# A gated attention block on one core: both MLP products as seven-product block products

## The chip, the cores and the metric

The kernel is one program on one NeuronCore of a Trainium2 chip; the other cores are idle. The metric is the time of one execution in device microseconds. Of the core's engines, PE does the matmuls, DVE (vector) and ACT (scalar) read and write both SBUF and the eight PSUM banks, POOL (GpSimd) works on SBUF only, and SP issues the DMA transfers.

## The reference

One decoder layer over 1024 tokens (SEQ) of 1024 channels (D), all in float32. First comes a mixing half: RMS norm, projections, differential attention and a pooling mixer, gates, and an output projection `w_o`, added to `x`. The MLP follows:

```python
h2 = rms_norm(x, norm2_g[l])
u = jnp.square(jax.nn.relu(jnp.einsum('bsd,df->bsf', h2, w_mlp_in[l])))
x = x + jnp.einsum('bsf,fd->bsd', u, w_mlp_out[l])
```

The inner width FF is 4096, so each MLP product is 1024 x 1024 x 4096.

## The kernel before

**Precision.** Each float32 operand is kept as two float32r parts: `hi` is the copy that ACT writes, and `lo` is the rest, which DVE gets by subtracting (`split_hi` L495, `split_lo` L776). `passes` (L1135) makes three matmuls of each pair: hi x hi, lo x hi, hi x lo. Each matmul has 128x128 weights and 512 moving columns and adds into one PSUM bank.

**Output projection.** `out_projection(t)` (L1378) handles one tile of 128 tokens: 2 halves of output columns x 8 blocks of k x 3 matmuls. Its operand is `featT`, the split of `mergedT`: ACT's `merged_hi` (L701), DVE's `merged_lo` (L1055), and POOL for the first tile (L488). DVE adds the result to the residual `res` (L1082), which lies in SBUF as 8 tiles loaded from x. ACT squares it (L734), POOL makes the inverse root (L413, L415), DVE the norm `h2_row` (L1094), and PE transposes it (`h2_transpose` L1395) two tiles later; ACT and DVE split the transposed tile into `featT` (L728, L1074).

**MLP.** FF is cut into 8 chunks of 4 blocks of 128. `mlp_up(c)` (L1413) computes, for each block j and each half i of the tokens, 8 blocks of k x 3 matmuls. ACT applies Relu and Square (L754, L759), DVE squares once more and takes the low part (L1103, L1106); the result `uT` stays in SBUF. `mlp_down(c)` (L1430) computes, for each tile of tokens and each half of output columns, 4 blocks x 3 matmuls, and DVE adds them to `res` (L1116). The weights come in blocks of 512 KB through four `raw` tiles (`load` L316, `load_chunk` L339) and are split once (L500, L779).

**Order.** Each engine has its own queue, written out by hand, with loops over chunks; semaphores connect them. SP's queue is in order too, so a transfer behind a wait goes out only when the wait ends.

Of the kernel before, what the change touches and what calls it, by code (L numbers as in the profile page):

```python
# [24 lines left out]
F32 = mybir.dt.float32  # L25
F32R = mybir.dt.float32r
# [8 lines left out]
def trunk_layer(nc, x, norm1_g, w_in, b_gate, q_norm_g, k_norm_g, lam_params, subln_g,  # L35
# [33 lines left out]
    with ExitStack() as ctx:  # L69
# [50 lines left out]
        res = at("res", 64, [P, T, D])  # L120
        h2_row = [at(f"h2_row{i}", 144 + 4 * i, [P, D]) for i in range(2)]
        g2_row = at("g2_row", 152, [P, D])
        square2 = at("square2", 156, [P, D])

        uT = (at("uT_hi", 144, [P, CH, SEQ], F32R), at("uT_lo", 96, [P, CH, SEQ], F32R))
        relu = [at(f"relu{i}", 208 + 2 * i, [P, HT]) for i in range(2)]
        u_full = [at(f"u_full{i}", 212 + 2 * i, [P, HT]) for i in range(2)]
# [7 lines left out]
        in_hi = at("in_hi", 128, [P, 2, BLOCK], F32R)  # L135
        in_lo = at("in_lo", 136, [P, 2, BLOCK], F32R)
        slots = [(slot_hi[:, i], slot_lo[:, i]) for i in range(4)]
        slots += [(more_hi[:, i], more_lo[:, i]) for i in range(4)]
        slots += [(in_hi[:, i], in_lo[:, i]) for i in range(2)]
# [36 lines left out]
        def sem(name):  # L176
# [7 lines left out]
        res_in = sem("res_in")  # L184
# [130 lines left out]
        def _(sp):  # L315
# [22 lines left out]

            def load_chunk(c):  # L339
                for i, (kind, j) in enumerate(MLP_ORDER):  # L340
                    if kind == "in":
                        load(i % 4, mlp_in_v[:, :, bass.ds((c * CH + j) * P, P)], MLP0 + 8 * c + i)
                    else:
                        load(i % 4, mlp_out_v[:, bass.ds(c * CH + j, 1), :], MLP0 + 8 * c + i, parts=1)
# [36 lines left out]
            sp.wait_ge(up_full, 4 * KD)  # L381
            for t in range(T):
                sp.dma_start(res[:, t, :], x_rows[t]).then_inc(res_in, 16)
# [4 lines left out]
            load_chunk(0)  # L388
            with sp.Fori(1, CHUNKS) as c:
                load_chunk(c)  # L390
            for t in range(T):
                sp.wait_ge(y_added, 2 * T * (CHUNKS - 1) + 2 * t + 2)
                sp.dma_start(y_rows[t], res[:, t, :]).then_inc(y_out, 16)
# [3 lines left out]
        def _(pool):  # L397
# [87 lines left out]

            for i, tiles in enumerate((slice(0, KD - 1), slice(KD - 1, KD))):
                pool.wait_ge(m_hi, i + 1)
                pool.tensor_tensor(featT[1][:, tiles, 0:P], mergedT[:, tiles, 0:P], featT[0][:, tiles, 0:P],  # L488
                                   ALU.subtract).then_inc(m_first, 1)
            for t in range(T):  # L490
                x_inverse(t, r_squared, r_mean, r_inv)

        @block.scalar
        def _(act):
# [214 lines left out]
            act.wait_ge(merged_ready, 2 * KD - 1)  # L709
# [3 lines left out]
            act.wait_ge(merged_ready, 2 * KD)  # L713
# [4 lines left out]
            for t in range(1, T):  # L718
                merged_hi(t)

            def chunk_hi(c, kind, j, used, used_n):
                i = mlp_pos[kind, j]
                split_hi(MLP0 + 8 * c + i, i % 4, raw_loads[i % 4] + 2 * c + 2 + i // 4, mlp_slot(kind, j), used, used_n)

            def h2_hi(t):
                for b in range(2):
                    act.wait_ge(h2T_full, 2 * t + b + 1)
                    nc.scalar.activation(featT[0][:, 4 * b:4 * b + 4, t * P:(t + 1) * P],  # L728
                                         k4(bank[:, 4 + 2 * (t % 2) + b, :], 4), ACT.Copy).then_inc(h2T_hi, 1)

            for t in range(T):
# [745 lines left out]
```

## Time and profile before

| | us |
|---|---|
| runs | 1386.84 (median), 1385.25, 3499.99 |
| span of the profiled execution | 1386.0 |
| PE busy | 1353.9 (98%) |
| DVE busy | 617.6 (45%) |
| ACT busy | 410.9 (30%) |
| POOL busy | 138.9 (10%) |
| mean DMA rate | 53 GB/s |

The profiled execution lasted 1386.0 us from its first to its last instruction. Busy shares are averages over stages with different limits. The mixing half takes the first 586 us, the output projection stands from there to 685, and the MLP from there to 1382. A group of the profile gives the busy time of all its instructions and the mean length of one; matmuls overlap, so their lengths add up to more than the time.

### The profile page before, as it was taken

The page shows a single profiled execution, that of the slowest core. Times are in us where ns is not written, and L with a number is a line of the kernel's source. Part 1 is how long each engine was busy: PE and PEld are TensorE (multiplying, and loading weights), DVE is VectorE, ACT ScalarE, POOL GpSimd, SP SyncE. Part 2 cuts the span into 40 slices and gives each one's busy share as a digit, 9 for nine tenths or more (in the row PEclk, how much of TensorE's full clock was granted, in tenths as well). Part 3 has the DMA queues.
Part 4 walks back from the last instruction along what each step waited for, and adds up shares of the span by engine and source line. Part 5 has one row for each costly group of instructions (what it writes and reads, how often), then busy time and mean ns, then how long its engine had stood idle before and what let it go on. Part 6 is the DMA issues. An engine that isn't in the chain of part 4 may idle for free.

```text
span 1386.0 us, 18136 instructions
## 1 busy us (share of the span) xinstructions
PE 1353.9 (98%) x6537; PEld 1135.4 (82%) x6537; DVE 617.6 (45%) x1039; ACT 410.9 (30%) x801; POOL 138.9 (10%) x279
## 2 busy tenths in 40 slices
PE   5999999998999999999999999999999999999998
PEld 5888888886788888878888888888888888888887
DVE  5777777788322222253343342433424334243332
ACT  5565655564211111232230220302203022030120
POOL 3333333335000000000000000000000000000000
PEclk9999999999999999999999999999999999999999
DMA  8010101011111111161021120211202012021002
GB/s 247 16 47 16 46 15 45 8 31 31 46 46 49 57 45 46 61 228 31 0 91 31 46 76 15 76 30 45 76 15 76 30 45 76 9 78 33 30 17 105
DMA packets 86371, 73.20 MB, mean 53 GB/s; under 512 B 2477, under 2 KB 76866, under 8 KB 86338
## 3 DMA queue, kind: packets, MB, share of 16 engines
q1 hardware_dynamic: 86338, 72.77, 16.7%
q8 instruction: 20, 0.33, 0.1%
q14 instruction: 13, 0.11, 0.0%
HBM read 68.56 MB, written 4.19 MB: 52 GB/s over the span
## 4 chain that ended last, share of the span: by engine, by line
PE 91%; DVE 4%; issue 2%; ACT 1%; DMA 1%; POOL 0%; SPq 0%; DVEq 0%; ACTq 0%; POOLq 0%
PE bank L1139 84%; PE bank L1307 2%; PE bank L1236 1%; PE bank L1195 1%; DVE slot_lo L779 1%; DMA raw<-in_w_in 1%; PE bank L1403 1%; PE bank L1290 0%; DMA raw<-in_w_o 0%; ACT slot_hi L500 0%; DVE wT_lo L870 0%; DVE small L863 0%; DVE mixT_lo L996 0%; DVE featT_lo L794 0%; PE bank L1157 0%
## 5 line engine op out<-in xcount | busy, mean ns | idle before, releaser
L1139 PE MATMUL bank<-featT_hi,in_hi 128*128 128x512 f32 x512 | 199.4, 389 | 0.0
L1139 PE MATMUL bank<-featT_lo,in_hi 128*128 128x512 f32 x512 | 199.2, 389 | 0.0
L1139 PE MATMUL bank<-featT_hi,in_lo 128*128 128x512 f32 x512 | 199.2, 389 | 0.0
L1139 PE MATMUL bank<-slot_hi,uT_hi 128*128 128x512 f32 x512 | 199.2, 389 | 0.0
L1139 PE MATMUL bank<-slot_hi,uT_lo 128*128 128x512 f32 x512 | 199.2, 389 | 0.0
L1139 PE MATMUL bank<-slot_lo,uT_hi 128*128 128x512 f32 x512 | 199.2, 389 | 0.0
L1116 DVE TENSOR_TENSOR res<-res,bank 128x512 f32<-128x512 f32 x128 | 87.9, 687 | 233.9 <-PE bank L1139 233.9
L500 ACT ACTIVATE slot_hi<-raw 128x1024 fp32r<-128x1024 f32 x77 | 79.5, 1044 | 289.6 <-PE bank L1139 285.9
L779 DVE TENSOR_TENSOR slot_lo<-raw,slot_hi 128x1024 fp32r<-128x1024 f32 x77 | 94.3, 1229 | 144.6 <-ACT slot_hi L500 144.0
L1103 DVE TENSOR_TENSOR u_full<-relu 128x512 f32<-128x512 f32 x64 | 44.3, 692 | 196.7 <-ACT relu L754 196.7
L1139 PE MATMUL bank<-featT_hi,slot_hi 128*128 128x512 f32 x320 | 126.7, 396 | 0.0
L1139 PE MATMUL bank<-featT_lo,slot_hi 128*128 128x512 f32 x320 | 124.7, 390 | 0.0
L1139 PE MATMUL bank<-featT_hi,slot_lo 128*128 128x512 f32 x320 | 124.6, 389 | 0.0
L1139 PE MATMUL bank<-slot_hi,featT_hi 128*128 128x384 f32 (+1 forms) x320 | 119.0, 372 | 4.9 <-DVE slot_lo L779 3.1
L1139 PEld LDWEIGHTS bank<-featT_lo,in_hi 128*128 128x128 f32 x512 | 96.1, 188 | 20.0
L1139 PEld LDWEIGHTS bank<-slot_hi,uT_lo 128*128 128x128 f32 x512 | 96.1, 188 | 20.0
L1139 PEld LDWEIGHTS bank<-slot_lo,uT_hi 128*128 128x128 f32 x512 | 96.1, 188 | 19.9
L1139 PEld LDWEIGHTS bank<-slot_hi,uT_hi 128*128 128x128 f32 x512 | 96.1, 188 | 19.9
L1139 PEld LDWEIGHTS bank<-featT_hi,in_lo 128*128 128x128 f32 x512 | 96.1, 188 | 19.8
L1139 PEld LDWEIGHTS bank<-featT_hi,in_hi 128*128 128x128 f32 x512 | 96.1, 188 | 19.8
L1139 PE MATMUL bank<-slot_lo,featT_hi 128*128 128x384 f32 (+1 forms) x320 | 112.2, 351 | 0.0
L1139 PE MATMUL bank<-slot_hi,featT_lo 128*128 128x384 f32 (+1 forms) x320 | 112.0, 350 | 0.0
(146 smaller groups left out, 1965.3 us busy)
## 6 DMA issues: line engine op xcount, KB each, us to landing
raw<-in_w_mlp_in SPq DMA_DIRECT2D x32, 512.0 KB, 4.5
raw<-in_w_mlp_out SPq DMA_DIRECT2D x32, 512.0 KB, 3.4
raw<-in_w_in SPq DMA_DIRECT2D x28, 512.0 KB, 4.1
x_tile<-in_x SPq DMA_DIRECT2D x8, 512.0 KB, 4.7
res<-in_x SPq DMA_DIRECT2D x8, 512.0 KB, 9.2
out_y<-res SPq DMA_DIRECT2D x8, 512.0 KB, 2.6
raw<-in_w_o SPq DMA_DIRECT2D x7, 512.0 KB, 3.8
raw<-in_w_in SPq DMA_DIRECT2D x8, 256.0 KB, 4.8
```

The source lines that it names most:

```text
L500: nc.scalar.activation(slot[0][:, 0:width], raw[r][:, 0:width], ACT.Copy).then_inc(w_hi, 1)
L779: nc.vector.tensor_tensor(slot[1][:, 0:width], raw[r][:, 0:width], slot[0][:, 0:width], ALU.subtract).then_inc(w_ready, 1)
L1103: nc.vector.tensor_tensor(u_full[q % 2][:], relu[q % 2][:], relu[q % 2][:], ALU.mult).then_inc(u_sq_ready, 1)
L1116: nc.vector.tensor_tensor(res[:, t, half], res[:, t, half], bank[:, 4 + (2 * t + i) % 4, :], ALU.add).then_inc(y_added, 1)
L1139: mm = nc.tensor.matmul(out, a, b, start=start and i == 0, stop=stop and i == len(steps) - 1)
L1195: mm = nc.tensor.transpose(bank[:, b, k * P:(k + 1) * P], w_tok[:, (4 * c + k) * P:(4 * c + k + 1) * P], ident[:])
L1236: mm = nc.tensor.matmul(bank[:, 2 * c + p0 // 512, 0:p1 - p0], a, b, start=i == 0, stop=i == 2)
L1307: mm = nc.tensor.matmul(*m, start=k == 0 and i == 0, stop=k == t and i == 1)
L1403: mm = nc.tensor.transpose(bank[:, 4 + 2 * (t % 2) + b, k * P:(k + 1) * P], h2_row[t % 2][:, kk * P:(kk + 1) * P], ident[:])
```

## The change

Let A be the left operand, cut into halves of tokens and of the inner dimension, and B the right one, cut into halves of the inner dimension and of the output. The four block products of the result used to need eight products of halves; now they are formed from seven products of sums of halves, in Winograd's arrangement, with their additions before and after.

- *Up* (D x FF): FF is taken in 16 pairs of 128-column blocks. For each pair, DVE forms four sums of weight quarters (`t_sums`), ACT and DVE split all seven right operands, PE runs `product` seven times with 4 blocks of k x 3 matmuls of 512 columns, and DVE combines the seven banks with seven additions (`up_add`) into c11, c21, c22, c12 (two 128-column blocks by two token halves); ACT applies Relu and Square. The seven left operands (`LEFT`: three parts of h2, and four sums) are made once, in `h2_split_hi` and `h2_split_lo`: 11 DVE operations of 512 elements for each two tiles.
- *Between*: POOL forms four sums of the activations, and SP stores seven tiles of 256 KB per pair in DRAM (`u_store`).
- *Down* (FF x D): the inner dimension is taken in 4 quarters, each with 7 products (28 in all). Product n loads 1 MB from `u_store` (`load_s`), uses one of the seven forms of the quarter of `w_mlp_out` (`load_o`: four blocks of 1 MB; `o_sums` on POOL: four sums of 2048 elements), has both operands split over 2048 elements by ACT and DVE (`down_hi`, `down_lo_o`, `down_lo_s`), and is 4 tiles of tokens x 4 x 3 matmuls. DVE adds each tile to `acc`, `shared` or `p7_acc` (`down_add`), with a second addition for D1 and D5; POOL adds the shared sums at the end.
- *Residual*: `res` is now three tiles; each is stored in DRAM (`res_store`) after the addition and read back into `acc` (8 x 512 KB) before the down products.
- Token tiles go in the order 4, 0, 5, 1, 6, 2, 7, 3. `h2_row` is one tile, and `h2_transpose(s)` stands after the first half of `out_projection(s + 1)`.
- The loops of this part are written out.

`apart` and `wait` are as before. The core of the diff, with 12 columns of indentation taken off; removed lines and empty ones are left out:

```diff
+sp.wait_ge(merged_ready, 2 * KD)
+load_res(0)
+load_res(1)
+sp.wait_ge(w_ready, WO + 7)
+load_res(2)
 sp.wait_ge(m_split, T - 1)
 sp.wait_ge(m_first, 2)
 sp.dma_start(g2_row[:], norm2_g.to_broadcast([P, D])).then_inc(g2_in, 16)
+load_pair(0)
+for s in range(T):
+    sp.wait_ge(res_ready, 2 * s + 2)
+    sp.dma_start(res_store[ORDER[s]], res[s % 3][:]).then_inc(res_out[s % 3], 16)
+    if s + 3 < T:
+        sp.wait_ge(h2_ready, s + 1)
+        sp.wait_ge(res_out[s % 3], 16 * (s // 3 + 1))
+        load_res(s + 3)
+    if s == 5:
+        sp.wait_ge(h2_ready, s + 1)
+        sp.wait_ge(res_out[2], 32)
+        load_pair(1)
...
+def load_s(n):
+    c, q = divmod(n, 7)
+    sp.wait_ge(u_out[q], 16 * 4 * (c + 1))
+    wait(sp, d_tile, 4 * (n - 2))
+    sp.dma_start(s_raw[n % 3][:], u_store[q, 4 * c:4 * c + 4].rearrange("q p c -> p q c")).then_inc(s_in[n % 3], 16)
+def load_o(c, b):
+    rows = mlp_out_v[:, 8 * c:8 * c + 8, :].rearrange("p (q two) c -> p two q c", two=2)
+    sp.dma_start(o_raw[c % 2][b][:], rows[:, b // 2, :, HALVES[b % 2]]).then_inc(o_in[c % 2][b], 16)
+for p in range(PAIRS):
+    if p + 2 < PAIRS:
+        sp.wait_ge(t_ready, 7 * (p + 1))
+        load_pair(p + 2)
+    if p == PAIRS - 1:
+        sp.wait_ge(t_ready, 7 * PAIRS)
+        sp.wait_ge(p_done, 7 * (PAIRS - 1))
+        load_o(0, 0)
+        load_s(0)
+        load_o(0, 3)
+    sp.wait_ge(u_ready, 4 * p + 1)
+    store_u(D1, p, u_tile[0])
...
+    for i, q in enumerate((D7, D5, D6)):
+        sp.wait_ge(s_ready, 4 * p + 1 + i)
+        store_u(q, p, s_tile[i])
+    if p == PAIRS - 1:
+        sp.wait_ge(p_done, 7 * p + P7 + 1)
+        load_o(0, 1)
+        sp.wait_ge(p_done, 7 * PAIRS)
+        load_s(1)
+        load_s(2)
+        for i in range(3):
+            sp.wait_ge(res_out[i], 16 * (3 - i // 2))
+        for t in range(QN):
+            sp.dma_start(acc[:, t, :], res_store[t]).then_inc(acc_in[0], 16)
+        load_o(0, 2)
+        for t in range(QN, T):
+            sp.dma_start(acc[:, t, :], res_store[t]).then_inc(acc_in[1], 16)
+    sp.wait_ge(u_ready, 4 * p + 4)
+    store_u(D2, p, u_tile[3])
+    sp.wait_ge(s_ready, 4 * p + 4)
+    store_u(D3, p, s_tile[3])
+for i in range(7):
+    sp.wait_ge(u_out[i], 16 * PAIRS)
+for n in range(2, DOWN):
+    c, i = divmod(n, 7)
+    if c + 1 < QUARTERS and 2 <= i < 6:
+        wait(sp, d_tile, 28 * c)
+        load_o(c + 1, (3, 1, 0, 2)[i - 2])
+    if n > 2:
+        load_s(n)
...
+u11, u21, u22, u12 = u_tile
+for p in range(PAIRS):
+    pool.wait_ge(u_ready, 4 * p + 2)
+    wait(pool, u_out[1], 16 * p)
+    pool.tensor_tensor(s_tile[0][:], u11[:], u21[:], ALU.subtract).then_inc(s_ready, 1)
+    pool.wait_ge(u_ready, 4 * p + 3)
+    wait(pool, u_out[4], 16 * p)
+    pool.tensor_tensor(s_tile[1][:], u21[:], u22[:], ALU.add).then_inc(s_ready, 1)
...
+act.wait_ge(merged_ready, 2 * KD)
...
+for p in range(PAIRS):
+    more = p + 1 < PAIRS
+    if more:
+        for i in range(5):
+            t_split_hi(p + 1, i)
+    else:
+        down_hi(0)
+    act.wait_ge(p_done, 7 * p + P1 + 1)
+    if p == 0:
+        act.wait_ge(res_out[0], 48)
+    else:
+        act.wait_ge(relu_done, 4 * (p - 1) + 1)
+    nc.scalar.activation(c11[:], bank[:, product_bank(p, P1), :], ACT.Copy).then_inc(first_copied, 1)
+    relu_square(p, 0)
+    if more:
+        t_split_hi(p + 1, 5)
+        t_split_hi(p + 1, 6)
+    relu_square(p, 1)
+    relu_square(p, 2)
+    relu_square(p, 3)
+for n in range(1, DOWN):
+    down_hi(n)
...
+def t_sums(p):
+    b11, b12, b21, b22 = (b_quarter(p, q) for q in range(4))
+    f = pair_f[par]
+    dve.wait_ge(pair_in[par], 16 * (p // 2 + 1))
+    if p > 1:
+        dve.wait_ge(p_done, 7 * (p - 1))
+    nc.vector.tensor_tensor(f[:, P5], b12, b11, ALU.subtract).then_inc(t_f, 1)
+    dve.wait_ge(t_f, 4 * p + 1)
+    nc.vector.tensor_tensor(f[:, P6], f[:, P5], b22, ALU.subtract).then_inc(t_f, 1)
+    dve.wait_ge(t_f, 4 * p + 2)
+    nc.vector.tensor_tensor(f[:, P4], b21, f[:, P6], ALU.add).then_inc(t_f, 1)
+    nc.vector.tensor_tensor(f[:, P7], b22, b12, ALU.subtract).then_inc(t_f, 1)
+def t_split_lo(p, i):
+    f = pair_f[par]
+    src = (f[:, P5], f[:, P4], b_quarter(p, 0), f[:, P6], b_quarter(p, 2), f[:, P7], b_quarter(p, 3))[i]
+    dve.wait_ge(t_hi, 7 * p + i + 1)
+    nc.vector.tensor_tensor(pair_lo[par][:, i], src, pair_hi[par][:, i], ALU.subtract).then_inc(t_ready, 1)
...
+for s in range(T):
+    add_res(s, 0)
+    if s == T - 1:
+        t_sums(0)
+    if s > 0:
+        h2_split_lo(s - 1)
+    if s == T - 1:
+        t_split_lo(0, 0)
+    add_res(s, 1)
+    if s == T - 1:
+        t_split_lo(0, 1)
+    h2_norm(s)
+for i in (2, 3):
+    t_split_lo(0, i)
+h2_split_lo(T - 1)
+for i in (4, 5, 6):
+    t_split_lo(0, i)
+for p in range(PAIRS):
+    more = p + 1 < PAIRS
+    p5, p4, p1, p6, p2, p7, p3 = (bank[:, product_bank(p, i), :] for i in range(7))
+    if more:
+        if p == 0:
+            dve.wait_ge(wo_full, 2 * T)
+        t_sums(p + 1)
+        for i in range(5):
+            t_split_lo(p + 1, i)
+    else:
+        down_lo_o(0)
+        down_lo_s(0)
+    def up_add(i, out, psum, other):
+        nc.vector.tensor_tensor(out[:], psum, other[:], ALU.add).then_inc(up_sum, 1)
+    dve.wait_ge(first_copied, p + 1)
+    dve.wait_ge(p_done, 7 * p + P6 + 1)
+    if p == 0:
+        dve.wait_ge(res_out[0], 48)
+    else:
+        dve.wait_ge(relu_done, 4 * (p - 1) + 4)
+        dve.wait_ge(u_ready, 4 * (p - 1) + 4)
+    up_add(1, c21, p6, c11)
+    dve.wait_ge(up_sum, 7 * p + 1)
+    if p == 0:
+        dve.wait_ge(res_out[1], 48)
+    up_add(2, c12, p5, c21)
+    dve.wait_ge(p_done, 7 * p + P2 + 1)
+    up_add(3, c11, p2, c11)
+    if more:
+        t_split_lo(p + 1, 5)
+        t_split_lo(p + 1, 6)
+    dve.wait_ge(p_done, 7 * p + P7 + 1)
+    up_add(4, c22, p7, c21)
+    dve.wait_ge(up_sum, 7 * p + 4)
+    up_add(5, c21, p4, c22)
+    dve.wait_ge(up_sum, 7 * p + 5)
+    up_add(6, c22, p5, c22)
+    dve.wait_ge(p_done, 7 * p + P3 + 1)
+    up_add(7, c12, p3, c12)
...
+for n in range(DOWN):
+    if n + 2 < DOWN:
+        down_lo_o(n + 2)
+    down_add(n, 0)
+    down_add(n, 1)
+    if n + 2 < DOWN:
+        down_lo_s(n + 2)
+    down_add(n, 2)
+    down_add(n, 3)
...
+for s in range(T):
+    out_projection(s, 0)
+    if s > 0:
+        h2_transpose(s - 1)
+    out_projection(s, 1)
+LO, HI = slice(0, HT), slice(HT, SEQ)
+K1, K2 = slice(0, QK), slice(QK, KD)
+LEFT = (cut(featT, ALL, K2, HI), cut(featT, ALL, K1, HI), cut(featT, ALL, K1, LO), comb2,
+        cut(featT, ALL, K2, LO), comb3, comb4)
+LEFT_READY = (23, 23, 24, 27, 25, 26, 28)
+def product(p, i):
+    m = 7 * p + i
+    if p == 0:
+        pe.wait_ge(h2_lo, LEFT_READY[i])
+    pe.wait_ge(t_ready, m + 1)
+    if m < 4:
+        pe.wait_ge(res_ready, 2 * T - 3 + m)
+    elif m < 8:
+        pe.wait_ge(h2_f, 16)
+    else:
+        last_p, last_i = divmod(m - 8, 7)
+        if last_i == P1:
+            pe.wait_ge(first_copied, last_p + 1)
+        else:
+            pe.wait_ge(up_sum, 7 * last_p + SUM_FREES[last_i])
+    right = (pair_hi[p % 2][:, i], pair_lo[p % 2][:, i])
+    passes(bank[:, product_bank(p, i), :],
+           [(cut(right, ALL, k), (LEFT[i][0][:, k, :], LEFT[i][1][:, k, :])) for k in range(QK)]).then_inc(p_done, 1)
+for p in range(PAIRS):
+    for i in range(7):
+        if p == 0 and i == 2:
             h2_transpose(T - 1)
+        product(p, i)
+def down_product(n):
+    pe.wait_ge(d_lo, 2 * n + 2)
+    if n == 0:
+        pe.wait_ge(up_sum, 7 * (PAIRS - 1) + SUM_FREES[P5])
+        pe.wait_ge(first_copied, PAIRS)
+    if n == 1:
+        pe.wait_ge(up_sum, 7 * PAIRS)
+    right = (o_hi[n % 3], o_low(n))
+    left = (s_hi[n % 3], s_lo[n % 3])
+    for t in range(QN):
+        if n > 1:
+            pe.wait_ge(d_added, 4 * (n - 2) + t + 1)
+        cols = slice(t * P, (t + 1) * P)
+        passes(bank[:, 4 * (n % 2) + t, :],
+               [(cut(left, ALL, k, cols), cut(right, ALL, k)) for k in range(4)]).then_inc(d_tile, 1)
+for n in range(DOWN):
+    down_product(n)
```

## Rows read from the trace of the kernel before

**Rows 1.** The page: span and engine totals; the granted clock.
```profile
core 0: 1386.0 us, clock 0.997
PE 1353.9 (98%) x6537; PEld 1135.4 (82%) x6537; DVE 617.6 (45%) x1039; ACT 410.9 (30%) x801; POOL 138.9 (10%) x279
```

**Rows 2.** Groups by line and form, 691.3 to 1382 us: busy, mean ns | idle, releaser.
```profile
L1139 PE MATMUL bank<-slot_hi,uT_hi 128*128 128x512 f32 x512 | 199.2, 389 | 0.0
...
L1139 PE MATMUL bank<-featT_hi,in_hi 128*128 128x512 f32 x504 | 196.1, 389 | 0.0
...
L1116 DVE TENSOR_TENSOR res<-res,bank 128x512 f32<-128x512 f32 x127 | 87.2, 687 | 231.9 <-PE bank L1139 231.9
L1106 DVE TENSOR_TENSOR uT_lo<-u_full,uT_hi 128x512 fp32r<-128x512 f32 x64 | 44.3, 693 | 2.7
...
L759 ACT ACTIVATE uT_hi<-relu 128x512 fp32r<-128x512 f32 x64 | 40.5, 633 | 2.0
L779 DVE TENSOR_TENSOR slot_lo<-raw,slot_hi 128x1024 fp32r<-128x1024 f32 x32 | 39.1, 1222 | 4.6 <-ACT slot_hi L500 4.6
L754 ACT ACTIVATE relu<-bank 128x512 f32<-128x512 f32 x64 | 38.3, 599 | 225.1 <-PE bank L1139 225.1
...
L500 ACT ACTIVATE slot_hi<-raw 128x1024 fp32r<-128x1024 f32 x32 | 33.6, 1049 | 282.5 <-PE bank L1139 282.5
```

**Rows 3.** The chain of waits: start us, length us, what.
```profile
590.39 6.29 DMA raw<-in_w_o
...
599.08 25.05 PE bank L1139 x102
...
684.95 5.48 PE bank L1139 x24
...
691.31 690.90 PE bank L1139 x3048
...
1382.23 0.69 DVE res L1116
```

**Rows 4.** DVE in order of time: start, length, line, operation [idle before].
```profile
597.79 1.23 DVE L779 TENSOR_TENSOR more_lo<-raw,more_hi 128x1024 fp32r<-128x1024 f32 x1 [2.40 <-ACT more_hi L500]
598.94 8.03 DVE L1058 TENSOR_TENSOR featT_lo<-mergedT,featT_hi 128x1024 fp32r<-128x1024 f32 x7
607.34 1.29 DVE L1082 TENSOR_TENSOR res<-res,bank 128x512 f32<-128x512 f32 x2 [0.37 <-DMA res<-in_x]
611.09 1.28 DVE L1094 SCALAR_TENSOR_TENSOR h_row<-res,small,g_row 128x1024 f32<-128x1024 f32 x1 [2.46 <-DMA g_row<-in_norm_g]
...
613.27 0.69 DVE L1082 TENSOR_TENSOR res<-res,bank 128x512 f32<-128x512 f32 x1 [0.31 <-PE bank L1139]
616.20 1.28 DVE L1094 SCALAR_TENSOR_TENSOR h_row<-res,small,g_row 128x1024 f32<-128x1024 f32 x1 [2.23 <-POOL small L415]
...
697.42 0.69 DVE L1103 TENSOR_TENSOR u_full<-relu 128x512 f32<-128x512 f32 x1 [1.83 <-ACT relu L754]
698.16 0.69 DVE L1106 TENSOR_TENSOR uT_lo<-u_full,uT_hi 128x512 fp32r<-128x512 f32 x1
```

**Rows 5.** POOL and DVE in order of time, where both work on SBUF.
```profile
326.23 1.89 POOL L452 TENSOR_TENSOR wide_window<-wide_window 128x1022 f32<-128x1022 f32 x1
335.27 2.94 POOL L452 TENSOR_TENSOR wide_window<-wide_window 128x1022 f32<-128x1022 f32 x1
331.22 4.04 DVE L996 TENSOR_TENSOR mixT_lo<-window,mixT_hi 128x1024 fp32r<-128x1024 f32 x2
347.52 1.23 DVE L996 TENSOR_TENSOR mixT_lo<-wide_window,mixT_hi 128x1024 fp32r<-128x1024 f32 x1 [2.77 <-ACT mixT_hi L664]
```

**Rows 6.** Windows: length, busy PE, PEld, DVE, ACT, POOL, clock, DMA share, GB/s.
```profile
100.00:200.00 100.00, 99.15 (x638) 88.36 (x638) 76.68 (x196) 60.15 (x172) 37.16 (x84) 1.00 0.09 27
200.00:300.00 100.00, 99.48 (x628) 87.35 (x626) 73.52 (x176) 58.30 (x160) 36.26 (x79) 1.00 0.08 23
590.00:600.00 10.00, 7.60 (x33) 5.64 (x32) 6.07 (x6) 4.89 (x6) 0.00 (x0) 1.00 0.86 312
600.00:604.00 4.00, 4.00 (x13) 3.10 (x12) 4.00 (x5) 4.00 (x5) 0.00 (x0) 0.57 1.03 420
```

**Rows 7.** The page, DMA issues: count, KB each, median us from issue to landing.
```profile
raw<-in_w_mlp_out SPq DMA_DIRECT2D x32, 512.0 KB, 3.4
...
res<-in_x SPq DMA_DIRECT2D x8, 512.0 KB, 9.2
out_y<-res SPq DMA_DIRECT2D x8, 512.0 KB, 2.6
raw<-in_w_o SPq DMA_DIRECT2D x7, 512.0 KB, 3.8
```

More of the change, by code:

```diff
@@ L118, in trunk_layer @@
         gate = at("gate", 208, [P, 2, SEQ])
[L120 to L127, printed above, removed]
+        ORDER = (4, 0, 5, 1, 6, 2, 7, 3)
@@ L394, in _ @@
+            for t in range(QN):
+                sp.wait_ge(y_ready, t + 1)
+                sp.dma_start(y_rows[t], acc[:, t, :]).then_inc(y_out, 16)
             sp.wait_ge(y_out, 16 * T)
@@ L493, in _ @@
+            for i, p0 in ((D4, 0), (D5, 1)):
+                for t in range(QN):
+                    pool.wait_ge(d_added, last + 4 * i + t + 1)
+                    pool.wait_ge(folded, 2 * t + 1)
+                    pool.tensor_tensor(acc[:, QN + t, HALVES[p0]], acc[:, QN + t, HALVES[p0]], p7_acc[:, t, :],
+                                       ALU.add).then_inc(folded, 1)
         @block.scalar
@@ L1077, in _ @@
[L1077 to L1089 removed]
+            for s in range(1, T):
+                merged_lo(s)
@@ L1111, in down @@
-            def down(c, between=None):
-                for t in range(T):
-                    for i, half in enumerate(HALVES):
-                        n = 2 * T * c + 2 * t + i
-                        dve.wait_ge(down_full, n + 1)
-                        nc.vector.tensor_tensor(res[:, t, half], res[:, t, half], bank[:, 4 + (2 * t + i) % 4, :],
-                                                ALU.add).then_inc(y_added, 1)
-                    if t == 0 and between:
-                        between()
@@ new lines, in down_lo_s @@
+            def down_lo_s(n):
+                dve.wait_ge(d_hi, 2 * n + 2)
+                nc.vector.tensor_tensor(s_lo[n % 3][:], s_raw[n % 3][:], s_hi[n % 3][:], ALU.subtract).then_inc(d_lo, 1)
+            for s in range(T):
+                add_res(s, 0)
[6 more added lines that the diff above has]
+                add_res(s, 1)
+                if s == T - 1:
+                    t_split_lo(0, 1)
+                h2_norm(s)
@@ L1395, in h2_transpose, with out_projection @@
-            def h2_transpose(t):
-                pe.wait_ge(h2_ready, t + 1)
-                if t < 2:
+            def out_projection(s, i):
+                n = 2 * s + i
+                cols = slice(ORDER[s] * P, (ORDER[s] + 1) * P)
+                if i == 0:
+                    wait(pe, m_split, s)
+                if s == 0:
+                    pe.wait_ge(gate_ready, 4 * KD)
+                wait(pe, res_ready, n - 3)
+                for k in range(KD):
+                    if s == 0:
+                        if k % 2 == 0:
+                            pe.wait_ge(w_ready, WO + 4 * i + k // 2)
+                        pe.wait_ge(m_first, 1 + (k == KD - 1))
+                    w = (k4(slots[4 * i + k // 2][0], 2), k4(slots[4 * i + k // 2][1], 2))
+                    mm = passes(bank[:, n % 4, :], [(cut(featT, ALL, k, cols), cut(w, ALL, k % 2))],
+                                start=k == 0, stop=k == KD - 1)
+                mm.then_inc(wo_full, 1)
```

501 lines of the change are left out of this document (296 added, 205 removed).

## The prediction

> **What bounds the kernel now.** The clock and engine totals come first: the granted clock is full on average, and PE is busy for 98% of the span [rows 1]. The groups by line, cut to the MLP stage, show what PE does there: 3072 matmuls of 512 columns in two families of three, with DVE and ACT waiting for PE rather than the reverse [rows 2]. The chain of waits says it more sharply: one unbroken piece of 3048 matmuls, 690.90 us long, is followed only by a DVE addition and the last store [rows 3]. That is 690.90 / 3048 = 0.2267 us per matmul (the 389 ns of the groups are overlapped lengths; the pitch counts). With the first 24, in 5.48 us, the two MLP products are 3072 x 0.2267 = 696.4 us, half the span. What removes matmuls here removes time, as long as nothing else ends later.
>
> **The matmuls.** After: up 16 pairs x 7 products x 12, down 28 products x 4 tiles x 12, each 1344; 2688 in all, 384 fewer, with 128x128 weights and 512 moving columns as before. That is 384 x 0.2267 = **-87.0 us**. A product up lasts 12 x 0.2267 = 2.72 us, a pair 19.04, a product down 10.88. The vector work grows instead, so each of its loops is priced.
>
> **DVE in the up phase.** A 512-column addition or subtraction is 0.69 us [rows 2]; two independent ones follow at 0.60, two dependent ones at 0.74 [rows 4]. Per pair: `t_sums` 2.7; five splits 3.0; three `up_add` 2.0; then DVE waits for ACT, which does Relu 0.60, Square 0.63 and a split copy of 0.6 after the third addition: 1.9; two splits 1.3; four `up_add` 2.8. Sum 13.7 us against 19.04 of PE. POOL's four subtractions and additions are new. POOL's nearest row is 1.89 us for 1022 elements, about 1.1 for 512. When POOL and DVE both work on SBUF each gets longer: POOL 2.94 for 1.89, and two DVE subtractions 4.04 for 2.46 [rows 5]. The floor is that POOL's 4.4 us never meet DVE, the ceiling that they are added whole: 18.1. I take the ceiling; PE still paces, with 0.9 us to spare. The Trainium skill, SBUF — State Buffer, section "Who interferes with whom", says that a DVE instruction with two SBUF inputs and a GpSimd instruction that reads SBUF exclude each other for a whole instruction, and one with a PSUM input does not. By that rule the sum of 18.1 would stand as the ceiling, and part of POOL's work would fall beside the PSUM additions at no cost.
>
> Bank reuse has its own margin: product (p+1, 1) needs the sixth addition of pair p. P7 ends at 16.3, but DVE reaches the fourth addition only at about 18; the sixth ends near 20.3, and the bank is wanted at 21.8. ACT has some 10 us of work per pair. Nothing charged.
>
> **Transfers in steady state.** Up: seven 256 KB stores and a 1 MB load per 19 us; down: a 1 MB load per product and four more per quarter. Both are 150 GB/s on average. The trace shows 420 GB/s over 4 us [rows 6], so less than half is used. `load_s(n)` starts when product n-3 ends, two products (21.8 us) before it is wanted: 1 MB takes about 5 (4 KB rows of 512 KB land in 3.4 us, [rows 7]), ACT's copy of 2048 elements 1.9 and DVE's 2.3 (both from the 512 and 1024 rows of [rows 2]), behind DVE's queued 4 us. It has some 9 us left. DVE does 7.3 us per product, 10.1 in those with double additions, and POOL's four `o_sums` of about 3.5 us each per quarter (from the 1.89 of [rows 5]) could add 2.0 on average, against 10.88. Charged nothing; if this cover goes, every product down waits.
>
> **Start of the output projection.** The first tile is now number 4, in the second half of tokens, so ACT's last `merged_hi` waits for `merged_ready` 16 in place of 15 and the two weight copies behind it move by about 1.5 us. PE already waits here for `more_lo`, which waits for a 6.29 us transfer beside eight residual loads [rows 3, 4]. Only two residual loads are now beside it, and 512 KB of w_o take 3.8 [rows 7]. I set +1.5 against -2 and take 0; bounds -2 and +3.
>
> **The first transpose.** It used to come after two more row tiles; now it comes after `out_projection(1, 0)`. DVE ends the seven merged splits at 606.97, does two additions, and from the end of an addition to the norm are 2.24 us (ACT Square, then POOL), plus 1.28 of the norm; `g2_row` also lands at 611.1 [rows 4]. So h2 is ready near 612.3. PE, from 599.08 through the rest of tile 0 and 24 matmuls at partly half clock, is there at about 606.8: **+5.5 us**. A clock cost follows: in the trace, after a gap of 2 us, the granted clock is 0.57 over 4 us and 102 matmuls take 25.05 us where 23.12 would do, 1.9 more [rows 3, 6]. I charge **+1.9**. Bounds for both: 0 and 9.
>
> For the later tiles: the same chain is 0.69 + 2.24 + 1.28 = 4.3 us and 24 matmuls cover 5.44. Behind an odd tile DVE has eight splits and sums, about 6 us, which makes the addition 0.6 late, still inside. At nothing; without cover, 1 to 2 us per tile.
>
> **Into pair 0.** Transpose 7 comes after two products. Product 2 needs the first low part of it: copy, subtraction and two weight splits ahead in DVE's queue make PE wait 0.9. Product 3 needs four more DVE results, 1.6. DVE then starts pair 1's sums 5 us behind, and product (1, 1) waits 2.5 for its bank. **+5.0 us**, and 1 for a clock that may drop in a part of the cases. Bounds 1 and 9.
>
> **From up to down.** Times from the start of pair 15. The last D3 store of pair 14 stands ahead in SP's queue, so `load_o(0,0)`, `load_s(0)`, `load_o(0,3)` go out at about 5. Down product 0's splits then occupy ACT and DVE until 16.8, ahead of pair 15's own additions; the sixth addition ends at 21.1, PE is free at 19.04: 2.1 us. Product 1: SP passes `s_ready` 63 at about 25 and only then sends `load_o(0,1)`, `load_s(1)`, `load_s(2)`. At 370 GB/s for 2 KB rows (between the 312 and 420 of [rows 6]) s(1) lands at 32.8; behind ACT's copy (1.9) and DVE's (2.3) product 1 can start at 37.0, 5.0 after product 0 ends. Product 3: behind s(2) stand 4 MB of residual, a block of w_mlp_out, two stores, and two blocks of the next quarter that SP sends ahead of `load_s(3)`. From 25 these are 12.1 MB; at 370 to 420 GB/s some 32 us with a drain for the stores, so s(3) lands at 62.8 and product 3 can start at 67.0, where product 2 ends at 58.8: 8.2 us. **+15.3 us**, and two clock drops of 1.9, **+3.8**. Bounds: 5 and 28. The trace goes to 420 GB/s on 4 KB rows. The Trainium skill, DMA: Bandwidth & Descriptors, section "Specifications", gives an HBM limit of about 358 GB/s per core; by it the 4 MB of residual would take 1.6 us more, and the sum would be 1.6 higher. The measured row decides.
>
> **The end.** From the last matmul at 1382.2: one addition of 0.69 and a store whose issue and landing end the span [rows 3, 7]. It is the same after; POOL's folds lie beside products 25 to 27. Nothing.
>
> **Sum** against the profiled execution: 1386.0 - 87.0 + 0 + 5.5 + 1.9 + 5.0 + 1.0 + 15.3 + 3.8 = 1331.5. The median of three runs is 1386.84, 0.8 above the span, and so I predict **1332 us**. The bounds of the four joints together, not all at one end at once, allow 1314 to 1347.
>
> **Rivals.**
> - *DVE paces the up phase.* My cycle of 18.1 us has 0.9 of margin, made of short rows. For it: 0.1 us more for each of some twenty waits makes 20.2. Against: part of POOL's work falls beside PSUM additions. Price 1.2 x 16 = 19 us: 1351.
> - *The joints are hidden.* Waits of 1 to 2 us, no clock drop: 8 us in place of 32.5, 1308. For it: DMA reaches 420 GB/s [rows 6]. Against: `load_s(3)` is behind 12 MB at any rate.
> - *The round trip paces the down phase.* Decides if more than 14 us pass from the issue of `load_s(n)` to its landing. The 9.2 us of eight residual loads queued together [rows 7] is the worst that the trace shows. At 17 us, 3 x 25 = 75 us: 1407.
> - *Slower: PE pauses once per pair and product for 2 us and the clock falls each time.* Place: `t_ready`, `up_sum` and `d_lo` on PE. Each pause costs 2 + 1.9 [rows 6] and there are 16 + 28: 172 us, 1504. It beats the saving from 0.7 us lost per pair and product on top of the joints' 32.5 (54.5 / 44 = 1.2 for no change). For: the clock did fall after a single gap. Against: DVE's cycles stay under PE's, and between 100 and 300 us, with PE's short gaps (99.15 and 99.48 busy of 100), the clock is full [rows 6].
> - *It removes less than it says.* The pitch could rise with the new operands. Both families of shapes have one pitch now, so a small chance, taken in below.
>
> **Chances.** Forecast 0.56; DVE paces 0.18; joints hidden 0.14; round trip 0.05; slower 0.04; no saving 0.03. What one can tell from no change is about 2%, 1359 to 1415. DVE pacing gives a sixth of its chance to "within 2%". Faster 0.56 + 0.14 + 0.15 + 0.05 for milder forms of the other three = 0.90; within 0.07; slower 0.03. The range takes in the forecast, DVE pacing at 1351 and the upper part of hidden joints: 1312 to 1354.
>
> **What would show it.** Right: 2688 MLP matmuls at 0.227 us; a PE gap of about 5 us before the first h2 transpose; gaps before down products 1 and 3; full clock between. DVE pacing: PE waiting at every pair for DVE's additions and a pair longer than 19.1. Wrong: gaps that recur in each pair or product, or a pitch above 0.227.

## The result, and the profile after

| | before | after |
|---|---|---|
| median of the runs, us | 1386.49 (4 runs, one of them at 3499.99) | 1336.47 (1335.14 to 1337.97, 4 runs) |
| ratio of the fast runs | | 0.9637, 95% interval 0.9623 to 0.9652 |
| span of the profiled execution, us | 1386.0 | 1333.3 |
| mean granted clock | 0.997 | 0.989 |

The kernel is 3.6% faster; forecast were 1332 us and a range of 1312 to 1354. The ratio leaves out the run of 3499.99 us, a slow one. The totals, which answer to [rows 1]:

```profile
span 1333.3 us, 17609 instructions
PE 1273.8 (96%) x6153; PEld 1066.0 (80%) x6153; DVE 887.0 (67%) x1233; ACT 535.1 (40%) x937; POOL 356.3 (27%) x377
q1 hardware_dynamic: 106754, 139.88, 31.5%
```

PE has 384 fewer matmuls (6537 - 6153) and is still the busiest engine. DVE rose from 618 to 887 us, POOL from 139 to 356, and transfers from 72.8 to 139.9 MB, in the shade of PE. That shade is thinner than the shares suggest, as the experiments show.

Where did PE wait? Its operations in order of time, from 580 us on; only those that begin after a wait are shown (start, length, operation, in brackets the idle time before it and what ended it):

```profile
589.33 0.50 PE L1510 MATMUL bank<-slot_hi,featT_hi 128*128 128x512 f32 x1 [1.45 <-DVE slot_lo L1022]
596.23 0.50 PE L1510 MATMUL bank<-more_hi,featT_hi 128*128 128x512 f32 x1 [1.14 <-DVE more_lo L1022]
611.64 1.97 PE L1776 MATMUL bank<-ident,h_row 128*128 128x128 f32 x8 [6.94 <-DVE h_row L1355]
691.24 0.47 PE L1510 MATMUL bank<-featT_hi,pair_hi 128*128 128x512 f32 x1 [0.41 <-issue]
699.11 0.50 PE L1510 MATMUL bank<-featT_hi,pair_hi 128*128 128x512 f32 x1 [0.97 <-DVE featT_lo L1332]
702.89 0.50 PE L1510 MATMUL bank<-comb_hi,pair_hi 128*128 128x512 f32 x1 [0.73 <-DVE comb_lo L1344]
718.40 0.47 PE L1510 MATMUL bank<-featT_hi,pair_hi 128*128 128x512 f32 x1 [1.61 <-DVE c L1432]
1007.38 0.76 PE L1510 MATMUL bank<-o_hi,s_hi 128*128 128x512 f32 x1 [5.82 <-DVE c L1432]
1024.87 0.50 PE L1510 MATMUL bank<-o_hi,s_hi 128*128 128x512 f32 x1 [4.37 <-DVE s_lo L1397]
1055.46 0.80 PE L1510 MATMUL bank<-o_hi,s_hi 128*128 128x512 f32 x1 [6.96 <-DVE s_lo L1397]
```

There are ten waits, all where one stage meets the next: at the start of the output projection, before the first transpose, in pairs 0 and 1, and before down products 0, 1 and 3. Between 718 and 1001 us and from 1055 to the end PE never waits. The chain of waits ends like that of before [rows 3], with one long piece of matmuls; the windows answer to [rows 6] (clock, DMA share and GB/s are the last three columns):

```profile
1055.46 274.14 PE bank L1510 x1200
1329.62 0.69 DVE acc L1491
```

```profile
608.00:616.00 8.00, 4.36 (x15) 3.83 (x16) 3.17 (x4) 1.60 (x3) 0.74 (x2) 0.57 0.68 211
720.00:980.00 260.00, 260.00 (x1149) 215.27 (x1148) 214.79 (x246) 126.06 (x221) 90.82 (x56) 1.00 0.45 151
1004.00:1012.00 8.00, 4.62 (x12) 3.70 (x13) 3.80 (x6) 6.58 (x9) 3.84 (x4) 0.57 0.34 129
```

1149 matmuls in 260 us are 0.2263 us each, so the pitch is that of before. The granted clock is full in the stages and 0.57, mostly its lower level (1.2 of 2.4 GHz), around the waits of 5 to 7 us.

**The account.** From the last `mergedT` addition to the last matmul the kernel before takes 1382.21 - 587.40 = 794.8 us, this one 1329.60 - 586.03 = 743.6: 51.2 less. The matmuls give 87.0. The waits take 27.8 (6.94, then 3.72 for the four before 719, then 17.15 at the three down products); those inside tile 0 of the output projection are 2.6 for 2.4. Low clock takes 7.4 for 1.7 (PE's busy time in each 4 us window, times what its granted clock lacks to 1.00). 87.0 - 27.8 - 0.2 - 5.7 = 53.3. Of the other 2.1 some 1.3 is how a wait is counted: from the modelled end of a matmul, 0.39 after its start, where the next could start at 0.23. The rest, under 1 us, stays open.

### The profile page after: what moved, and what is told of

Its sections match the earlier page's. It is cut to its first block and busy times, and to the rows that moved or that the text cites. A ratio compares the mean times of both kernels' runs of the same rounds, so it can differ in the third digit from the quotient of the medians.

```text
span 1333.3 us, 17609 instructions
## 1 busy us (share of the span) xinstructions
PE 1273.8 (96%) x6153; PEld 1066.0 (80%) x6153; DVE 887.0 (67%) x1233; ACT 535.1 (40%) x937; POOL 356.3 (27%) x377
## 5 line engine op out<-in xcount | busy, mean ns | idle before, releaser
L1510 PE MATMUL bank<-o_hi,s_hi 128*128 128x512 f32 x448 | 176.8, 395 | 17.1 <-DVE s_lo L1397 11.3
L1510 PE MATMUL bank<-o_hi,s_lo 128*128 128x512 f32 x448 | 176.4, 394 | 0.0
L1510 PEld LDWEIGHTS bank<-o_hi,s_hi 128*128 128x128 f32 x448 | 85.6, 191 | 36.2 <-DVE s_lo L1397 12.2
L1510 PE MATMUL bank<-featT_hi,pair_hi 128*128 128x512 f32 x256 | 100.0, 391 | 3.0 <-DVE c L1432 1.6
L1397 DVE TENSOR_TENSOR s_lo<-s_raw,s_hi 128x2048 fp32r<-128x2048 f32 x28 | 84.5, 3016 | 25.5 <-ACT s_hi L992 25.5
L1510 PE MATMUL bank<-o_lo,s_hi 128*128 128x512 f32 x256 | 101.0, 395 | 0.0
L1510 PEld LDWEIGHTS bank<-o_hi,s_lo 128*128 128x128 f32 x448 | 85.5, 191 | 18.0
L1510 PE MATMUL bank<-featT_hi,pair_lo 128*128 128x512 f32 x256 | 99.6, 389 | 0.0
L1510 PE MATMUL bank<-featT_lo,pair_hi 128*128 128x512 f32 x256 | 99.6, 389 | 0.0
L1432 DVE TENSOR_TENSOR c<-bank,c 128x512 f32<-128x512 f32 x112 | 75.4, 688 | 18.2 <-PE bank L1510 16.0
```

The costliest lines, as they stand in the source:

```text
L1397: nc.vector.tensor_tensor(s_lo[n % 3][:], s_raw[n % 3][:], s_hi[n % 3][:], ALU.subtract).then_inc(d_lo, 1)
L1432: nc.vector.tensor_tensor(out[:], psum, other[:], ALU.add).then_inc(up_sum, 1)
L1510: mm = nc.tensor.matmul(out, a, b, start=start and i == 0, stop=stop and i == len(steps) - 1)
```

## The experiments

The code ahead of the change takes a little more or less from run to run: the matmul that ends the wait for `slot_lo` in the output projection stands at 589.1 to 591.5 us in eleven kernels that do not differ up to there. So beside the median the length of the stage is given, from that matmul to the end of the last one: 740.3 us in the changed kernel (589.33 to 1329.60). It comes from one execution of each kernel, and a wait that an edit does not touch differs between them too (5.82 before down product 0 in the changed kernel, 4.93 and 5.01 in the first two kernels below), so differences of 1 us are not read.

**The first transpose, later.**

```diff
-                if s > 0:
+                if s > 1:
                     h2_transpose(s - 1)
                 out_projection(s, 1)
+                if s == 1:
+                    h2_transpose(0)
```

> The first transpose of h2 goes behind the second half of out_projection(1) instead of the first; nothing else moves. Theory: PE's 6.94 us wait before it was for h_row, and 5.4 us of matmuls now stand in front of it; 1.5 us of the wait and the low clock after it are left or go too. DVE's second residual addition of tile 1 now waits behind the split of tile 4, which may cost up to 1 us at the next transpose. Expected 5 to 8 us less than the changed kernel: 1328.5 to 1331.5 us. Rival (the wait was hidden by later slack, since PE has other waits behind it): no change, 1336.

Measured: 1332.93 us, ratio 0.9622 (0.9604 to 0.9640); stage 736.7, 3.6 less. PE's waits around the transposes:

```profile
613.26 1.72 PE L1776 MATMUL bank<-ident,h_row 128*128 128x128 f32 x8 [1.99 <-DVE h_row L1355]
622.50 1.10 PE L1776 MATMUL bank<-ident,h_row 128*128 128x128 f32 x8 [1.05 <-DVE h_row L1355]
```

6.94 became 1.99 + 1.05, and the clock fell all the same (0.70 from 612 to 616, 0.88 to 620). The cause is right. The size, 5 to 8 us, was not reached: the second transpose took over part of the wait, and the low clock stayed.

**s(3) ahead of the stores and the next quarter.**

```diff
                     for t in range(QN, T):
                         sp.dma_start(acc[:, t, :], res_store[t]).then_inc(acc_in[1], 16)
+                    load_s(3)
...
-                if n > 2:
+                if n > 3:
                     load_s(n)
```

> SP sends load_s(3) behind the residual loads, ahead of the last two stores, of the wait for all stores and of the two blocks of the next quarter. Theory: the 6.96 us wait before down product 3 is due to that order; s(3) lands some 11 us earlier, the wait goes whole, and with it the low clock behind it (0.57 over the 8 us from 1052, about 1.7 us). Expected 8.5 us less: 1327 to 1329 us. Rival (DVE's queue at this joint is as late as the load: its splits run beside POOL's sums and take 4 to 5.5 us each): 2 to 4 us less, 1332 to 1334, with the wait for the low part of s still there.

Measured: 1330.92 us, 0.9607 (0.9584 to 0.9630); stage 732.8, 7.5 less. By the stage this is near the theory's 8.5. The median, 5.5 less, lies between the two forecasts; its four runs spread over 5.3 us. The wait before product 3 is gone, so DVE's queue was not as late as the load; 1.48 us stay before product 4:

```profile
1073.75 0.50 PE L1511 MATMUL bank<-o_hi,s_hi 128*128 128x512 f32 x1 [1.48 <-DVE s_lo L1398]
```

**The loads of the joint, earlier.**

```diff
-                if p == PAIRS - 1:
+                sp.wait_ge(u_ready, 4 * p + 1)
+                store_u(D1, p, u_tile[0])
+                if p == PAIRS - 2:
                     sp.wait_ge(t_ready, 7 * PAIRS)
                     sp.wait_ge(p_done, 7 * (PAIRS - 1))
                     load_o(0, 0)
                     load_s(0)
                     load_o(0, 3)
-                sp.wait_ge(u_ready, 4 * p + 1)
-                store_u(D1, p, u_tile[0])
+                if p == PAIRS - 1:
+                    sp.wait_ge(p_done, 7 * p + P7 + 1)
+                    load_o(0, 1)
+                    sp.wait_ge(p_done, 7 * PAIRS)
+                    load_s(1)
+                    load_s(2)
...
```

The same three lines of `load_o(0, 1)`, `load_s(1)` and `load_s(2)` with their waits are taken out behind the three stores.

> SP sends the first three loads of the down phase in pair 14, behind its first store, and the next three (one block of w_mlp_out, s(1), s(2)) in pair 15 behind its first store, not behind the stores that wait for POOL. Theory: the 5.82 us before down product 0 are DVE's additions of pair 15, which stand behind splits whose loads went out 7 us late; the 4.37 us before product 1 are s(1), issued late. Both go but for about 1 us, and 2 us of low clock: 10 to 12 us less, unless product 3 now waits longer for s(3), whose issue is bound to transfers that end at about the same time as before: then 4 to 7 us of it come back. Expected 1326 to 1332 us. Rival (the transfers pace this joint by their bytes, not their order): no more than 2 us less.

Measured: 1326.12 us, 0.9571 (0.9547 to 0.9595), as the theory has it; stage 729.3, 11.0 less. 5.82 and 4.37 became 0 and 1.22; the wait for s(3), which this edit leaves alone, is 7.39:

```profile
1016.02 0.50 PE L1511 MATMUL bank<-o_hi,s_hi 128*128 128x512 f32 x1 [1.22 <-DVE s_lo L1398]
1045.61 0.79 PE L1511 MATMUL bank<-o_hi,s_hi 128*128 128x512 f32 x1 [7.39 <-DVE s_lo L1398]
```

No byte is saved here, so order and not volume made the two waits that went.

**All three.**

> The three edits together. Theory: of 17.2 us of waits at the joint some 2 are left, of 6.9 at the first transpose at most 1.5, and the clock falls at most once: 6.9 + 17.2 + 5.5 of low clock - 4 = 25 us less, 1309 to 1315 us. Rival (bytes pace the joint): 1318 to 1326.

Measured: 1318.28 us, 0.9509 (0.9492 to 0.9526); stage 722.1, 18.2 less, in the rival's range and not in that of the theory. One wait is new, before product 4:

```profile
1049.28 0.79 PE L1512 MATMUL bank<-o_hi,s_hi 128*128 128x512 f32 x1 [4.80 <-DVE s_lo L1399]
```

SP's queue in that kernel shows why (start, length, issuing line, transfer):

```profile
1011.60 1.56 SPq L474 DMA_DIRECT2D s_raw<-u_store  x1
1013.21 2.44 SPq L467 DMA_DIRECT2D u_store<-u_tile  x1
1015.70 1.09 SPq L467 DMA_DIRECT2D u_store<-s_tile  x1
1028.14 1.49 SPq L479 DMA_DIRECT2D o_raw<-in_w_mlp_out  x3
1029.72 0.75 SPq L474 DMA_DIRECT2D s_raw<-u_store  x1
1030.51 1.68 SPq L479 DMA_DIRECT2D o_raw<-in_w_mlp_out  x1
```

After s(3) at 1011.60 SP waits until 1028 for all stores to land, which only the blocks of the next quarter need, and sends three blocks of 1 MB before s(4). Whether bytes pace the joint, as the rival says, can be tested: move s(4) alone.

**s(4) ahead of that wait as well.**

```diff
+            load_s(4)
             for i in range(7):
                 sp.wait_ge(u_out[i], 16 * PAIRS)
...
-                if n > 3:
+                if n > 4:
                     load_s(n)
```

> The three edits together, and load_s(4) goes out before the wait for all stores and the four blocks of the next quarter that stood ahead of it. Theory: with the three edits the one long wait left at the joint is 4.80 us before down product 4, for s(4), whose issue waited for the stores (until 1028) and then for four loads of 1 MB; it goes, with some 1.4 us of low clock: 5 to 6 us less than the three edits alone, 1311.5 to 1314 us. Rival (DVE beside POOL is late anyway, its split of 2048 elements takes 6.1 us there): 1 to 2 us less, 1316 to 1317.

Measured: 1312.39 us, 0.9472 (0.9452 to 0.9492); stage 714.9, 25.4 less than the changed kernel and 7.1 less than with three edits; the median is 5.9 less, inside the theory's range. The joint's waits are 1.21 and 0.39 us, the clock is full through it, and the transfers run at 391 GB/s where PE used to stand still:

```profile
1004.00:1012.00 8.00, 6.79 (x30) 5.30 (x30) 8.00 (x4) 5.06 (x3) 0.48 (x1) 1.00 1.02 391
```

All the bytes are still moved. So the order, not the volume, had cost 15.6 of the 17.2 us of waits at this joint.

**norm2_g earlier.** It is loaded into a free weight tile and copied by ACT when its place is free, on top of the last one.

```diff
+            sp.wait_ge(w_ready, WO + 4)
+            sp.dma_start(raw[0][:], norm2_g.to_broadcast([P, D])).then_inc(g2_in, 16)
...
+                    act.wait_ge(g2_in, 16)
+                    nc.scalar.activation(g2_row[:], raw[0][:], ACT.Copy).then_inc(g2_copied, 1)
```

> As the last one, and norm2_g is loaded some 12 us earlier into a free tile and copied by ACT once its place is free. Theory: the norm before the first transpose then waits for ACT's Square and POOL's root alone; its start moves from about 5.4 us behind the second addition to 2.3 to 3.4 us; the 1.96 us wait of PE before the first transpose goes and the clock stays up there: 2 to 4 us less, 1308 to 1311 us. Rival: the wait moves to the second transpose, whose own chain is as long: at most 1 us less.

Measured: 1309.57 us, 0.9458 (0.9435 to 0.9481); stage 714.7, 0.2 less. The wait before the first transpose is gone and stands before the second:

```profile
618.54 1.85 PE L1782 MATMUL bank<-ident,h_row 128*128 128x128 f32 x8 [2.10 <-DVE h_row L1361]
```

The median lies in the theory's range, but the stage says that the rival is right. Of the 2.8 us between the two medians, 2.4 lie ahead of the stage in the profiled executions (589.06 against 591.46), where the kernels do not differ (norm2_g goes out at 591.78), and the intervals overlap. This kernel and the last one are faster than the kernels before and after the change; between the two the runs don't decide.

**Is the up phase paced by PE? Two, then four more DVE operations per pair.**

```diff
                     for i in range(5):
                         t_split_lo(p + 1, i)
+                    for i in range(2):
+                        nc.vector.tensor_tensor(extra[i][:], b_quarter(p + 1, 1), b_quarter(p + 1, 0), ALU.subtract)
```

The second kernel has `range(4)`.

> Two more DVE subtractions of 512 elements per pair, into an unused place, behind the five splits. Theory: DVE's loop is shorter than PE's pair of 19.04 us by the 1.25 us that it waits for PE after its second addition, and the two extra ones take 2 x 0.60: absorbed, 0 to 1 us more, 1336 to 1338. Rival (DVE's chain already paces): +1.2 x 14 = 17 us, 1353.

> Four such subtractions per pair. Theory: 2.4 us against 1.25 us of margin: each pair gets 1.1 us longer, about 14 pairs show it, 12 to 17 us more, 1349 to 1354, and PE waits for DVE's additions in each pair. Rival (bank reuse gives 1.5 us more margin than DVE's own loop): no change in 14 pairs, at most 3 us.

Measured with two: 1341.75 us, 0.9676 (0.9659 to 0.9693); stage 743.4, 3.1 more. That is over the forecast of 0 to 1 us, and far from the rival's 17. No pair from 2 on waits, as the theory has it; what it missed is the wait before pair 1's second product, where DVE is still behind from pair 0. It grew from 1.61 to 2.79, and the clock fell behind it (0.84 and 0.74 in the two windows of 4 us from 720 on): 2.4 us together. Measured with four: 1354.86 us, 0.9767 (0.9749 to 0.9784), at the upper end of the forecast; stage 758.0, 17.8 more. Now every pair from pair 4 on waits:

```profile
783.28 0.47 PE L1513 MATMUL bank<-featT_hi,pair_hi 128*128 128x512 f32 x1 [0.69 <-DVE c L1435]
803.26 0.47 PE L1513 MATMUL bank<-featT_hi,pair_hi 128*128 128x512 f32 x1 [0.67 <-DVE c L1435]
...
1003.05 0.47 PE L1513 MATMUL bank<-featT_hi,pair_hi 128*128 128x512 f32 x1 [0.67 <-DVE c L1435]
```

(1003.05 - 783.28) / 11 = 19.98 us per pair, paced by DVE. Less the 2.4 us of the extra ones this is 17.6 us for DVE's own loop, against 19.04 of PE. So PE paces the up phase of the changed kernel, and 1.4 us more of DVE per pair would end that. The two extra ones agree: they took DVE's wait behind its second addition from 1.25 us to 0.17.

**What POOL takes of it.** Four extra operations, and POOL fills its four tiles with zeros; the four sums of the activations are left out.

```diff
-                pool.tensor_tensor(s_tile[0][:], u11[:], u21[:], ALU.subtract).then_inc(s_ready, 1)
+                pool.memset(s_tile[0][:], 0.0).then_inc(s_ready, 1)
```

> As with four extra subtractions, and POOL fills its four tiles per pair with zeros instead of adding and subtracting activations (this leaves out the four sums of the activations). Theory: POOL's reads of SBUF are what stretches four to five of DVE's operations per pair by about 4.1 us in all (0.69 to 1.67); a fill reads nothing, so DVE's loop falls to about 16 us with the extra ones, and the time is that of the changed kernel, 1334 to 1337. Rival (any POOL work on SBUF stretches DVE): as with four extra alone, 1349 to 1354.

Measured: 1338.25 us, 0.9644 (0.9627 to 0.9662), 1.3 us above the forecast and far from the rival; stage 743.0, 15.0 less than with four extra alone and 2.7 more than the changed kernel. The waits of pairs 4 to 15 are gone. The wait before pair 1's second product stays at 4.01 for 1.61: up to there POOL has no such work, and DVE has the four extra operations all the same. DVE's and POOL's operations in the changed kernel:

```profile
850.99 1.67 DVE L1368 TENSOR_TENSOR pair_f<-pair_f,pair_raw 128x512 f32<-128x512 f32 x1
852.69 1.67 DVE L1370 TENSOR_TENSOR pair_f<-pair_raw,pair_f 128x512 f32<-128x512 f32 x1
854.28 1.78 DVE L1371 TENSOR_TENSOR pair_f<-pair_raw 128x512 f32<-128x512 f32 x1
```

```profile
850.44 1.67 POOL L634 TENSOR_TENSOR s_tile<-u_tile,u_tile 128x512 f32<-128x512 f32 x1 [12.26 <-ACT u_tile L976]
852.06 1.75 POOL L637 TENSOR_TENSOR s_tile<-u_tile,u_tile 128x512 f32<-128x512 f32 x1
853.89 1.62 POOL L640 TENSOR_TENSOR s_tile<-u_tile,s_tile 128x512 f32<-128x512 f32 x1
```

The first of the three with POOL's fills:

```profile
858.76 0.69 DVE L1369 TENSOR_TENSOR pair_f<-pair_f,pair_raw 128x512 f32<-128x512 f32 x1
```

Four to five of DVE's operations per pair are stretched by POOL's reads, in all by 4.1 us (1.67, 1.67 and 1.78 for 0.69 each, 2.38 for two at 1.28). Each of the three shown ends 0.55 us after POOL's beside it, less than its own 0.69: it stood nearly still while POOL's ran. POOL pays as well, with 6.6 us for four operations that take 1.3 each without DVE. POOL's fills of 0.53 us fall beside the same operations and stretch none. The Trainium skill, SBUF — State Buffer, section "Who interferes with whom", separates the two cases in this way: a DVE instruction with two SBUF inputs contends with a GpSimd instruction that reads SBUF and not with one that only writes it. Both halves agree with these rows.

**The same matmuls as before, with all the new work.** The product P1 of each pair and D1 of each quarter is computed twice.

```diff
+                if i == P1:
+                    passes(bank[:, product_bank(p, i), :],
+                           [(cut(right, ALL, k), (LEFT[i][0][:, k, :], LEFT[i][1][:, k, :])) for k in range(QK)])
                 passes(bank[:, product_bank(p, i), :],
...
+                    if n % 7 == D1:
+                        passes(bank[:, 4 * (n % 2) + t, :],
+                               [(cut(left, ALL, k, cols), cut(right, ALL, k)) for k in range(4)])
```

> One product per pair and one per quarter is computed twice into the same bank, so that PE makes the 3072 MLP matmuls of the kernel before with all the new work of the other engines. Theory: PE paces, so 384 x 0.2267 = 87.0 us more; the repeated first product of the quarter covers the waits before products 1 and 3 (11.3 us and their low clock), so 73 to 78 us more: 1409 to 1415 us. Rival (other engines or transfers pace part of the phases): less than 65 us more.

Measured: 1405.24 us, 1.0136 (1.0117 to 1.0154); stage 807.5, 67.2 more than the changed kernel. This is under the forecast and above the rival. The trace accounts for it: the repeated products also give DVE time at product 0 and in pair 1, so the waits at the down products and in pair 1, 18.8 us in all, are 4.9 here (1.77 before product 0, 1.08 before 3 and 2.05 before 4), and no low clock follows them. 87.0 - 13.9 = 73.1; some 5 us of low clock at the down joint are gone too, which leaves 68 against 67.2 measured. PE's pace carries the whole of the rest. With as many matmuls as before, the new scheme is 1.4% slower than the kernel before: that is what its extra work still costs where the repeated products cover most of it.

## Why the prediction was right

- *The matmuls, -87.0.* Right: 384 fewer at the same pitch, and the repeated products give it back.
- *DVE paces nothing.* Right, and the size too: DVE's loop is 17.6 us by the experiment, 13.5 of its own and 4.1 that POOL adds, where the prediction had 13.7 and, at the ceiling, 4.4. The two 4s agree in part by luck: POOL's four operations took 6.6 us and not 4.4, and DVE paid for a part of them. None fell beside DVE's PSUM additions, which end at 850.27 where POOL begins at 850.44. That such an addition is not stretched shows in the down phase, where two of them lie inside one of POOL's and take what two take alone:

```profile
1053.42 6.43 POOL L659 TENSOR_TENSOR o_raw<-o_raw,o_raw 128x2048 f32<-128x2048 f32 x1 [0.17 <-POOL o_t L659]
1055.33 1.27 DVE L1491 TENSOR_TENSOR acc<-acc,bank 128x512 f32<-128x512 f32 x2
```

- *The output projection's start, 0.* Right: 2.6 us of waits for 2.4. The sum left out that the low clock of the kernel before (1.7 us from 600 on) did not come back here.
- *The first transpose, 5.5 and 1.9 of clock.* Right in cause: 6.94 us, and 2.0 of clock. `g2_row` was 4.9 us on its way and landed after POOL's root. The 1.4 us more are PE's: it was there at 604.7, not at 606.8.
- *Into pair 0, 5.0 and 1.0 of clock.* 3.7 at the places named, and the clock did not fall there.
- *From up to down, 15.3 and 3.8.* 17.15 and 5.4. One term was mis-sized: product 0 was put at 2.1 us and waited 5.82. Pair 15 started at 982.4. POOL began 1.4 us later, its four operations took 1.3 us each where 1.1 had been taken, and behind them stands the last store, so the three loads went out at 990.2, 7.8 us after the start and not 5. The first block took 6.2 us to land, where about 5 had been taken. DVE's splits ended at 1003.3, 20.9 after the start, where 16.8 was forecast. Products 1 and 3 were put at 5.0 and 8.2 and waited 4.37 and 6.96.
- *Product 3's arithmetic.* It does not add up as written: 25 and "some 32 us" are 57, which would leave 2.4 us of wait; the 62.8 that was used has 5.8 us more that no term explains. The chain of waits shows what fills the time. From the first of these loads at 1012.2 to the landing of s(3) at 1049.0 are 36.8 us, of which SP stood 13.6 for the last store:

```profile
1024.83 13.62 DMA u_store<-s_tile
...
1038.50 0.38 SPq L479
...
1039.53 9.50 DMA s_raw<-u_store
...
1049.04 1.92 ACT s_hi L992
...
1050.99 4.43 DVE s_lo L1397
```

- *Bandwidth at the joint.* Over the 16 us from 1016 on, the transfers ran at 399 GB/s, inside the 370 to 420 that the sum used and above the 358 quoted beside it.
- *The sum.* 1331.5 for the span, measured 1333.3. This is closer than its parts. Too small were the first transpose (1.4), the joint to the down phase (1.9) and its clock (1.6); too large were pair 0 (1.3), its clock (1.0), and the start's low clock that went (1.7). The way in which waits are counted and the open rest add 2.1, and 1.4 us were won ahead of the stage. That these cancel to 1.8 is luck. The profiled execution lasted 1335.14 us by its time, 1.8 above its span, as every execution on record with a span is by 1.8 or 1.9. The prediction had added 0.8, from a median and a span of different executions. It is also the shortest of four, which is the rest of the way to 1336.47.
- *Rivals.* DVE pacing: refuted, though 2.4 us more per pair bring it about. Hidden joints at 1308: not what this order of transfers does, but 1312.4 is reached once SP's queue is put in order and the first transpose moved. Its argument against, 12 MB ahead of `load_s(3)`, was about order and not about bandwidth. Round trip: `load_s` took 5.6 us to land in the median and 13.5 at most, at the joint, where the rival wanted more than 14 each time. Recurring pauses and a longer pitch: nothing of them in the trace.

## What to carry to other kernels

When arithmetic is traded for vector work and transfers, price each loop against the engine that it hides behind, and then price each joint between stages apart: here the loops cost nothing and the joints, with the clock that fell at them, took some 33 of the 87 us. At a joint, read the queue of the engine that issues transfers: a load behind a store or behind a wait that it does not need is late by what it never depended on, and moving such loads, together with one transpose, gave back 25 us of the stage without saving a byte. An engine at 80% busy may have only 1.4 us of margin per loop, since others stretch it; add known work to it until the bound engine waits, and the margin is measured.

## What was not expected

- In these kernels the length of a wait between 1.7 and 3.5 us does not tell whether the clock falls. It fell after 1.97 us in the kernel before, and after 1.96, 1.99, 2.10 and 2.16 before the transposes in four of the kernels here. It stayed at 1.00 after 1.77 and 2.05 with the repeated products, and after the waits of 1.45 and 1.14 us at the start of the output projection. It stayed at 1.00 even after one of 3.44 before down product 1, in the kernel with POOL's fills. It fell after 2.79 and after each wait of 4 us and more. Waits of 0.67 us once per 20 us, with four extra DVE operations, left it at 1.00 from 780 to 1000 us.
- POOL's additions over 2048 elements took 4.5 to 6.5 us, where 3.5 had been estimated from 1.89 for 1022; DVE's splits of s, also over 2048, took 3.0 on average and up to 6.3, where 2.3 had been taken. The down phase has enough margin to hide both.
